# First gather by column halves, two late states in row quarters, and the order of the work around them

## The reference, cut to what matters

```python
for l in range(2):
    # mixer: u, q, k, v, g = rmsnorm(x) @ w_in ; pooling over windows, and retention with 4 heads of 128
    #   retention state of a sample sequence and head:  s_new = s0 * gamma**8 + (k * k_decay).T @ v
    #   x += [pool | silu(g) * groupnorm(o)] @ w_out
    # hierarchical MoE: the best of 4 groups, then the best 2 of its 4 experts
    for e in range(16):
        act = silu(hf @ w_gate[e]) * (hf @ w_up[e])          # hf = rmsnorm(x), w_gate/w_up: 1024 x 256
        y = y + (act * gates[:, e:e + 1]) @ w_down[e]        # w_down: 256 x 1024
    x = x + y
return rmsnorm(x), ..., new_ret_sample   # (2, 8, 4, 128, 128): s_new of each layer, sequence and head
```

## Time and profile before

| | before |
|---|---|
| median of 3 runs | 810.37 us (810.21 to 812.56) |
| the profiled execution's own time | 810.1 us |
| its span | 808.3 us |
| granted TensorE clock, mean | 0.996 |
| PE busy | 792.4 us (98%) |
| DVE busy | 601.0 us (74%) |
| ACT busy | 478.4 us (59%) |
| POOL busy | 331.7 us (41%) |
| chain that ended last: PE, DVE, issue, DMA | 55%, 29%, 8%, 6% |

### The profile page before, as it was taken

One profiled execution on the slowest core, in us unless ns is written; L12 is line 12 of the kernel. 1 busy time (PEld: TensorE's weight loads), 2 busy tenths in 40 slices (PEclk: granted clock), 3 DMA queues, 4 the chain that ended last, 5 costly groups with the idle time before them and its releaser, 6 DMA issues.

```text
span 808.3 us, 11933 instructions
## 1 busy us (share of the span) xinstructions
PE 792.4 (98%) x4092; PEld 628.5 (78%) x4092; DVE 601.0 (74%) x951; ACT 478.4 (59%) x816; POOL 331.7 (41%) x225
## 2 busy tenths in 40 slices
PE   9999999999999999999999999999999999999995
PEld 6887788878757888888588787888776678888861
DVE  5445655575789999999754456646658899999986
ACT  5633333612578888887663432444335798888874
POOL 0015996310042355664100199925012234656530
PEclk9999999999999999999999999999999999999998
DMA  8832223224959999998753322222379699999967
GB/s 295 288 117 66 78 66 118 105 79 150 409 187 386 375 362 377 398 370 296 273 187 104 86 73 71 66 80 91 99 296 346 240 416 347 387 377 396 342 226 287
DMA packets 57295, 188.17 MB, mean 233 GB/s; under 512 B 10862, under 2 KB 11886, under 8 KB 49036
## 3 DMA queue, kind: packets, MB, share of 16 engines
q1 hardware_dynamic: 44476, 156.56, 53.7%
q0 software_dynamic: 10368, 23.09, 7.7%
q10 hardware_dynamic: 2400, 7.87, 2.6%
HBM read 172.99 MB, written 29.39 MB: 250 GB/s over the span
## 4 chain that ended last, share of the span: by engine, by line
PE 55%; DVE 29%; issue 8%; DMA 6%; ACT 2%; DVEq 0%; SPq 0%; POOL 0%; ACTq 0%; POOLq 0%
PE ps L499 13%; PE ps L503 10%; PE ps L502 10%; DVE gul L2198 9%; DVE dnl L2203 7%; DVE hgTl L2214 4%; PE ps L501 3%; DMA back<-y_d 2%; PE ps L1483 2%; PE ps L1485 2%; PE ps L1484 2%; DVE y L2223 2%; DMA y_d<-y,rowidx 2%; PE ps L1462 2%; DVE act L2235 1%
## 5 line engine op out<-in xcount | busy, mean ns | idle before, releaser
L911 POOL DMA_INDIRECT y_d<-y,rowidx x32 | 118.2, 3695 | 121.6 <-DVE y L2223 114.5
L499 PE MATMUL ps<-wh,hT 128*128 128x512 f32 x408 | 163.5, 401 | 0.2
L2198 DVE TENSOR_TENSOR gul<-wgu,eh 128x1024 fp32r<-128x1024 f32 x128 | 150.7, 1222 | 0.1
L2189 DVE SCALAR_TENSOR_TENSOR wl<-raw,gcol,wh 128x512 fp32r<-128x512 f32 x80 | 78.5, 983 | 75.8 <-ACT wh L1133 75.7
L1164 ACT ACTIVATE eh<-wgu 128x1024 fp32r<-128x1024 f32 x128 | 128.5, 1057 | 4.0 <-PE ps L1485 3.9
L503 PE MATMUL ps<-wh,lT 128*128 128x512 f32 x313 | 122.4, 391 | 0.0
L502 PE MATMUL ps<-wl,hT 128*128 128x512 f32 x313 | 121.9, 390 | 0.0
L1483 PE MATMUL ps<-eh,hgTh 128*128 128x512 f32 x240 | 96.6, 402 | 0.4 <-issue 0.4
L1485 PE MATMUL ps<-eh,hgTl 128*128 128x512 f32 x240 | 93.8, 391 | 0.0
L1484 PE MATMUL ps<-gul,hgTh 128*128 128x512 f32 x240 | 93.5, 389 | 0.0
L1133 ACT ACTIVATE wh<-raw,gcol 128x512 fp32r<-128x512 f32 x80 | 57.3, 719 | 60.3 <-PE ps L501 56.2
(11 more groups left out here) (277 smaller groups left out, 1612.6 us busy)
## 6 DMA issues: line engine op xcount, KB each, us to landing
wgu<-in_gate_up SPq DMA_DIRECT2D x64, 1024.0 KB, 12.3
wdn<-in_w_down SPq DMA_DIRECT2D x64, 512.0 KB, 14.3
raw<-in_w_in SPq DMA_DIRECT2D x79, 256.0 KB, 2.7
raw<-in_w_out SPq DMA_DIRECT2D x32, 256.0 KB, 3.0
back<-y_d SPq DMA_DIRECT2D x16, 512.0 KB, 6.1
s<-in_state_ret POOLq DMA_DIRECT2D x8, 512.0 KB, 4.1
xn_d<-xf ACTq DMA_DIRECT2D x8, 512.0 KB, 7.6
x_in<-in_x_cols SPq DMA_DIRECT2D x8, 288.0 KB, 4.9
```

The lines of the kernel that those rows point to most:

```text
L499: pe.matmul(out, both, w_h, start=first, stop=False)
L911: pool.indirect_dma_start(out=y_d, out_offset=bass.IndirectOffsetOnAxis(ap=rowidx[:, 1, e:e + 1], axis=0), in_=y[s][:, :], in_offset=None, ...
L2189: ve.scalar_tensor_tensor(out=wl[S % SPL][:, :], in0=raw[S % RAW][:, :], scalar=gcol[:, 0, L, s % KC:s % KC + 1], in1=wh[S % SPL][:, :].bi ...
L2198: ve.tensor_tensor(gu_pair(gul, gul3, e, s, p), gu_pair(wgu, wgu3, e, s, p), gu_split(e, p)[:, :].bitcast(F32), ALU.subtract).then_inc(glo, 1)
```

## The change

- The rows of expert 0 are gathered in two column halves, by an index `halfidx` of their own (twice the row number, plus the half), written by DVE before `rowidx`. PE transposes the first half on its arrival, does the products of its first two blocks, and transposes the second half then.
- The updates of the two late states come in row quarters: values and keys of head 2 lie in partitions 0 to 63 and those of head 3 in 64 to 127, and each of the four products contracts 32 rows. Masks are per four sequences (`seqm4`). Two identity products stand ahead of the table products, one semaphore step covers all four updates, and 11 idle matmuls follow instead of 1.
- ACT does one late state ahead of the exponentials and three behind; the Silu table is loaded behind the rows of expert 0 and two pairs of expert 1. In expert 0 it copies the first rows of expert 1 ahead of a weight pair.
- DVE makes two low parts of expert 0's weights ahead of its wait for the exponentials.
- SP issues the gate and up weights of expert 3 right behind the first gather, ahead of the state stores.

```diff
-        kd_late = tile("kd_late", [P, NH - LATE, P], off=wpool_at)
+        kd_late = tile("kd_late", [P, P], off=wpool_at)
-        vb = [tile(f"vb{i}", [P, DECB, P], off=(d_at, d_at + 4096, gn_at, d_at + 4096)[i]) for i in range(NH)]
+        vb = [tile(f"vb{i}", [P, DECB, P], off=d_at + 4096 * i) for i in range(LATE)]
+        v_late = tile("v_late", [P, 4, P], off=gn_at + 2048)
...
                 sp.wait_ge(gat[0], 16 * used(L, 0, 0))
+                load_gu(L, AHEAD, 0)
                 for j in (1, 0):
-                    sp.wait_ge(s_late, 4 * L + (4, 3)[j])
+                    sp.wait_ge(s_late, 4 * L + (4, 2)[j])
                     sp.dma_start(o["new_ret_sample"][L, LATE + j], s_out[j][:, :, :]).then_inc(late_st, 16)
                 for s in range(3):
                     sp.wait_ge(gat[s], 16 * used(L, s, 0))
                 sp.wait_ge(late_st, 64 * (L + 1))
-                load_gu(L, AHEAD, 0)
                 load_dn(L, AHEAD, 0)
...
+            def gather_half(e, half, sem):
+
+                cols = slice(512 * half, 512 * half + 512)
+                pool.indirect_dma_start(out=hg[e % 3][:, cols], out_offset=None, in_=xn_d.rearrange("r (h d) -> (r h) d", h=2),
+                                        in_offset=bass.IndirectOffsetOnAxis(ap=halfidx[:, half:half + 1], axis=0),
+                                        bounds_check=half_bound, oob_is_err=False).then_inc(sem, 16)
...
+                pool.wait_ge(sg_done, NT * (L + 1))
+                pool.wait_ge(o_mm, NT * L + LAST)
+                seqm = c("seqm4").unsqueeze(2).to_broadcast([P, 4, P])
                 for h in range(LATE, NH):
-                    if h == 3:
-                        pool.wait_ge(on_tr, NT * L + 5)
-                    pool.tensor_tensor(vb[h][:, :, :], over(zq(LAST, "v")[:, h * P:(h + 1) * P], DECB),
-                                       c("seqm").unsqueeze(2).to_broadcast([P, DECB, P]), ALU.mult).then_inc(vb_done, 1)
+                    last = pool.tensor_tensor(v_late[NSAMP * (h - LATE):NSAMP * (h - LATE) + NSAMP, :, :],
+                                              over(zq(LAST, "v")[0:NSAMP, h * P:(h + 1) * P], 4), seqm[0:NSAMP], ALU.mult)
...
-                pool.wait_ge(tidx_done, L + 1)
-                for e in range(3):
+                pool.wait_ge(tidx_done, 2 * L + 1)
+                gather_half(0, 0, gat_left)
+                gather_half(0, 1, gat[0])
+                pool.wait_ge(tidx_done, 2 * L + 2)
+                for e in (1, 2):
                     gather(e)
...
+                if first(e):
+                    rows_hi(L, 1, (0,))
                 if not final(e):
                     gu_hi(L, e + 1, (s + 1) % 3, n[2], range(2 if first(e) else 0, 3))
-                if first(e):
-                    rows_hi(L, 1, (0,))
...
                 gu_hi(L, 0, 0, 0)
-                late_state(L, 2, 0)
                 late_state(L, 3, 0)
                 sc.wait_ge(most_done, L + 1)
-                sc.activation(gex[:, :, :], gds[:, :, :], ACT.Exp).then_inc(exp_out, 1)
-                sc.activation(small[:, 6:8, :], small[:, 4:6, :], ACT.Exp).then_inc(exp_out, 1)
-
-                table(ACT.Silu)
+                sc.activation(gex[:, :, :], gds[:, :, :], ACT.Exp).then_inc(by_act, 1)
+                sc.activation(small[:, 6:8, :], small[:, 4:6, :], ACT.Exp).then_inc(by_act, 1)
+
                 late_state(L, 3, 1)
+                late_state(L, 2, 0)
                 late_state(L, 2, 1)
                 sc.wait_ge(xn_st, 16 * NT * (L + 1))
                 rows_hi(L, 0)
                 gu_hi(L, 1, 1, 0, range(2))
+                table(ACT.Silu)
...
                 for k in range(4):
                     if first(e) and k == 2:
+                        pe.wait_ge(gat[0], 16 * used(L, 0, 0))
+                        rows_t(0, t_mm, halves=(1,))
                         pe.wait_ge(hg_hi, rows_split(L, e, 0))
...
-            def late_new(L, h, n):
-
-                pe.wait_ge(vb_done, NH * L + h - LATE + 1)
-                pe.matmul(ps[B_LATE[h - LATE][n]][:, :], kd_late[:, h - LATE, :], vb[h][:, 4 * n:4 * n + 4, :],
-                          start=False, stop=True).then_inc(skv_mm, 1)
+            def late_new(L):
+
+                pe.wait_ge(vb_done, 3 * L + 1)
+                for h in range(2):
+                    for n in range(2):
+                        rows = slice(NSAMP * h + 32 * n, NSAMP * h + 32 * n + 32)
+                        last = pe.matmul(ps[B_LATE[h][n]][:, :], kd_late[rows, :], v_late[rows, :, :], start=False, stop=True)
+                last.then_inc(skv_mm, 1)
...
-                late_new(L, 2, 0)
-
-                pe.wait_ge(names_p, L + 1)
+                late_old(L, *LATE_STEPS[1])
+                late_old(L, *LATE_STEPS[2])
+
+                pe.wait_ge(by_act, 3 * L + 1)
                 pe.wait_ge(names_b, 2 * L + 1)
...
-                for h, n in LATE_STEPS[1:]:
-                    late_old(L, h, n)
-                    late_new(L, h, n)
-                idle_turns(3, 1)
-
-                pe.wait_ge(gat[0], 16 * used(L, 0, 0))
-                rows_t(0, t_mm, pair=True)
+                late_old(L, *LATE_STEPS[3])
+                late_new(L)
+                idle_turns(3, 11)
+
+                pe.wait_ge(gat_left, 16 * (L + 1))
+                rows_t(0, t_mm, pair=True, halves=(0,))
...
             ve.wait_ge(tab_mm, L + 1)
+            for half in range(2):
+                last = ve.tensor_scalar(halfidx[:, half:half + 1], ps[2][:, 0:1], 2.0, 2.0 * NO_ROW + half, ALU.mult, ALU.add)
+            last.then_inc(tidx_done, 1)
...
-            ve.wait_ge(exp_out, 2 * L + 2)
+            gu_lo(L, 0, 0, range(2))
+            ve.wait_ge(by_act, 3 * L + 3)
...
-            gu_lo(L, 0, 0, range(3))
+            gu_lo(L, 0, 0, (2,))
```

More of the change, by code:

```diff
@@ L206, in build @@
         rowidx = tile("rowidx", [P, 2, NE], U32)
+        halfidx = tile("halfidx", [P, 2], U32)
         tab = region + 4096 * 3
@@ L338, in build @@
         gu3_ld = [sem(f"gu3_ld{h}") for h in range(2)]; dn3_ld = [sem(f"dn3_ld{k}") for k in range(2)]
-        gat = [sem(f"gat{i}") for i in range(3)]
+        gat = [sem(f"gat{i}") for i in range(3)]; gat_left = sem("gat_left")
         early_ld = [sem("early_ld0"), sem("early_ld1")]
@@ L774, in _ @@
                 load_dn(L, 1, 1)
-                sp.wait_ge(vb_done, NH * L + NH - LATE)
+                sp.wait_ge(vb_done, 3 * L + 1)
                 sp.wait_ge(late_st, 64 * L + 32)
@@ L915, in _ @@
             row_bound = pool.to_reg(SEQ + NSAMP - 1)
+            half_bound = pool.to_reg(2 * (SEQ + NSAMP) - 1)
             y_bound = pool.to_reg(2 * TOK - 1)
@@ L951, in _ @@
                     gate_gain(L, t)
+                pool.wait_ge(sg_done, NT * (L + 1))
+                pool.wait_ge(o_mm, NT * L + LAST)
+                seqm = c("seqm4").unsqueeze(2).to_broadcast([P, 4, P])
                 for h in range(LATE, NH):
-                    if h == 2:
-                        pool.wait_ge(sg_done, NT * (L + 1))
-                        pool.wait_ge(o_mm, NT * L + LAST)
-                    if h == 3:
-                        pool.wait_ge(on_tr, NT * L + 5)
-                    pool.tensor_tensor(vb[h][:, :, :], over(zq(LAST, "v")[:, h * P:(h + 1) * P], DECB),
-                                       c("seqm").unsqueeze(2).to_broadcast([P, DECB, P]), ALU.mult).then_inc(vb_done, 1)
+                    last = pool.tensor_tensor(v_late[NSAMP * (h - LATE):NSAMP * (h - LATE) + NSAMP, :, :],
+                                              over(zq(LAST, "v")[0:NSAMP, h * P:(h + 1) * P], 4), seqm[0:NSAMP], ALU.mult)
+                    if h < NH - 1:
+                        link(last)
+                last.then_inc(vb_done, 1)
+                pool.wait_ge(vb_done, 3 * L + 1)
                 pool.wait_ge(gain_ld, 64 * L + 16)
@@ L1089, in late_state @@
             def late_state(L, h, n):
-                sc.wait_ge(skv_mm, 6 * L + LATE_STEPS.index((h, n)) + 1)
+                sc.wait_ge(skv_mm, 3 * L + 1)
                 sc.activation(s_out[h - LATE][:, 4 * n:4 * n + 4, :], ps[B_LATE[h - LATE][n]][:, :].rearrange("p (b e) -> p b e", b=4),
@@ L1119, in end_state @@
             def end_state(L, h):
-                sc.wait_ge(skv_mm, 6 * L + 4 + h + 1)
+                sc.wait_ge(skv_mm, 3 * L + h + 2)
                 for n in range(2):
@@ L1262, in key_decay @@
                     sc.wait_ge(kv_mm, LAST * L + t - 1)
+                n = tokens(t)
                 for h in range(NH):
-                    dst = kd_late[:, h - LATE, :] if t == LAST and h >= LATE else kd[t % 2][:, h, :]
-                    last = sc.activation(dst, zq(t, "k")[:, h * P:(h + 1) * P], ACT.Copy,
-                                         scale=c("kdec", 1 + NL)[:, 1 + L if t == LAST else 0, h:h + 1])
+                    late = t == LAST and h >= LATE
```

(16 more changed lines are left out.)

8 lines of the change are left out of this document (4 added, 4 removed).

## The result

The changed kernel takes 820.8 us (median of 6 runs, 817.02 to 824.02), the kernel before 810.4 us beside it. The ratio is 1.0119, interval 1.009 to 1.0148: **slower by 10 us**. Forecast was 809.4 us.

A forecast was written before the change was run, and what follows sets the result against it. PE and DVE, fully busy in 9.3 us expert periods, were taken as the bound, leaving only an earlier start: per layer -0.9 + 0.22 + 0.2 = -0.48 us, with 0.05 -1.0 us over two layers, giving 809.4 us; range 807.9 to 811.2.

The forecast's parts named there:

- The first gather by halves: Expert 0's gather, each layer: first half lands 3.46 us after its start, 0.9 us sooner; bounds 0 and 1.2 us.
- both estimates in the prediction: Earlier landing of the first half gather: 0.9 us from profiled traffic, 0.6 us by the Trainium skill's DMA rule.
- Rival (b): First gather's halves land no earlier, the price being rows and fixed steps: +0.4 us, 810.8 us; chance 0.17.
- The late states: PE before the experts: four row-quarter updates take 1.1 us, to 232.7, and with the idle matmuls cost nothing.
- rival (c): Late-state row quarters run one after another on PE, 3.4 us: +3.0 us in total, 813.4 us, slower; chance 0.06.
- The split's cost on PE: Expert 0's transposes and matmuls in two sets: 0.22 us given back before the third pair, bounds 0.1 and 0.4.
- ACT's order: Expert 1's row copy ahead of the third weight copy delays DVE's split of that pair: 0.2 us more lost.
- the DVE step: DVE subtraction at 248.57 in layer 0, 12.26 us after the gather's landing; forecast to come 0.5 us earlier.
- Every later step of the layer by the same: Sign: all steps after the DVE subtraction at 248.57 come earlier by the same 0.5 us, to the layer's end.
- rival (a): The whole shift is kept: half gather lands 1.2 us earlier, DVE finds slack; 2.5 us gained, 807.9 us; chance 0.14.
- SP: Fourth expert's gate and up weights leave near 237 instead of 242.46, stores land some 3 us later: gain or cost nothing.
- The prediction's own test: Any change in the experts' period of 9.3 us would break the argument altogether.

The follow-up runs named there:

- Experiment 7: experiment 6 with ACT's Silu table load between the first expert's row-copy halves and the second expert's third weight pair split before its first row copy: 811.25 us, ratio 1.0014.
- experiment 9: Experiment 7 with DVE's first two sums of returned rows moved later, behind its last down split and its last copy of y: 809.53 us, ratio 0.9982.
- the best version: The kernel of experiment 9, measured again unchanged against the kernel before: 810.19 us, ratio 0.9984.
- experiment 3: Changed kernel with the fourth expert's gate and up weights issued behind the two state stores but ahead of the wait for their landing: 812.01 us, ratio 1.0017.
- experiment 2: Kernel before with only the fourth expert's gate and up weights issued early, ahead of the state stores, and the wait that needs: 819.07 us, ratio 1.0131.
- experiment 4: Changed kernel with SP's wait for gathers and stores, and the down weights behind it, moved behind the next two experts' gate and up loads: 814.94 us, ratio 1.0061.
- experiment 5: Kernel before with two unused 32-byte SBUF blocks, so later tiles stand 32 or 64 bytes further on, no instruction changed: 810.34 us, ratio 0.9993.
- experiment 6: experiment 3 with tiles moved 32 bytes more, each a whole 64 bytes from its place in the kernel before, half indices in another tile: 810.21 us, ratio 0.999.

## Why the prediction was wrong, point by point

- **The first gather by halves: right.** Forecast 3.46 us to the landing, measured 3.38 and 3.41. That is 0.98 and 0.96 us sooner than the whole gather, more than both estimates in the prediction (0.9 and 0.6). Rival (b), no earlier landing, falls.
- **The late states: right.** Forecast 1.1 us for the four updates in row quarters, 232.7 for their end. The eight records of them in PE's timeline, and the idle matmuls behind, six of the eleven in this view (start us, us):

```profile
230.78 1.14 PE L1802 MATMUL ps<-v_late,kd_late 32*128 32x512 f32 x8
231.85 1.47 PE L1496 MATMUL ps<-still 128*128 128x512 bf16 x6
```

The next instruction starts 1.07 us after the first of them; rival (c), 3.4 us, falls. The clock stayed at 1.00.
- **The split's cost on PE: right.** In PE's timeline the third pair starts at 238.82, 7.72 us after the gather's start; the same view of before has it at 240.38, 8.43 us after. So the 0.7 us are there.
- **ACT's order: right in its place, too small.** Of the 0.7 us I let 0.2 be lost to the pair that ACT splits late. Lost was 0.65: the DVE step comes 16.56 us after the gather's start, before 16.62. DVE waited 0.75 us for that pair, and PE 0.35 for DVE. Experiment 7 got 0.6 us a layer back at this step by ACT's order and the table's place.
- **"Every later step of the layer by the same": wrong.** Experiments 7 and 9 show that a lead of 0.6 us ends at the rows that are loaded back. The 2.5 us of rival (a) never came either: the best version, with the two sums moved, gained about 1.4 us. The chain's 6% of DMA had 2% of `back<-y_d` in it, which the prediction did not look into.
- **SP: the step that failed.** The early weights and the late stores stood in the sum at nothing; they cost 3.1 us in layer 0 and 4.5 in layer 1. The prediction said that 2 MB sooner gain nothing, that the stores land some 3 us later, "then the down weights of that expert leave, 25 us before their use: nothing". The first was right (experiment 3). The second was low: the wait for the stores ended 8.9 us later than before, for in the changed kernel they landed 10.5 and 13.5 us after their issue, while before the queue went on 5.6 us after the second one's. The down weights left 8.0 us later than before. The third asked only whether the first transfer behind the wait was late. It was not; but four more stood behind it, and all that follow. I had read the DMA share of 0.99 as a sign that weights are never late. It says rather that hardly any lost DMA time can be made good there. Idle DMA engines at 250 us are idle ACT at 266 us. The prediction's own test, a change in the period of 9.3 us, is what came. Shown is that the order of weights and stores in SP's queue makes the loss (experiments 2 and 3); the blocked queue alone doesn't explain it, since half stayed when the next gate and up loads were let past (experiment 4).
- **A small addition.** The 0.05 us a period from the tiles' places was not foreseen, and the profile of before could not show it. Whether it reaches the total is open: experiment 5 says no, experiment 6 yes.

## What to carry to other kernels

Where a later stretch runs at a DMA share near 1, DMA time lost ahead of it can come back as waits there, even if the compute engines are all busy when it is lost: count the bytes moved up to its start, and ask of a moved transfer how long the queue is held behind it, not when its own data is used. Put small stores whose landing gates a queue ahead of large loads that gate nothing. And follow a gain at the front of a loop to the loop's end before it is summed: a wait there for something else can take it back, and then that consumer has to be moved too.

## What was not expected of the hardware

- Moving all tiles behind the constants by 32 bytes of SBUF, and those behind the row indices by 64, with no instruction changed (experiment 5), lengthened the down product's 12 matmuls an expert by 3 to 5 ns each (391 to 394, 389 to 394, 412 to 416), and the period from 9.31 to 9.36 us. With all of them moved by 64 bytes (experiment 6) it was 9.32 to 9.33. Why is not known. Weight loads (188 ns) and DVE's subtractions (1217 and 1211 ns) did not grow.
- Two stores of 512 KB issued 1.2 us behind 2 MB of loads on the same queue landed in 10.5 and 13.5 us. Without the loads ahead the queue that waits for both went on 5.6 us after the second one's issue, and with the loads behind them (experiment 3) they landed in 4.4 and 6.2 us.
